# Two-layer hybrid decoder step: norms and combinations tile by tile, ten gather buffers, tokens in five transfers, zeros written later

## The reference

```python
def rms_norm(x, g):
    y = xf * lax.rsqrt(jnp.mean(xf * xf, axis=-1, keepdims=True) + RMS_EPS)
    return (y * g).astype(x.dtype)

# layer 0: h += even_mixer(rms_norm(h, norm_mix_even));  h += hier_moe(rms_norm(h, norm_ffn[0]))
# layer 1: h += odd_mixer(rms_norm(h, norm_mix_odd));    h += hier_moe(rms_norm(h, norm_ffn[1]))
# y = rms_norm(h, norm_final)

def even_mixer(h, ...):      # conv and forgetting attention
    proj = jnp.einsum('ntd,de->nte', h, w_in)      # 1024 -> 2568 columns
    ...                                            # GLU, depthwise conv of width 31, attention
    return jnp.einsum('nte,ed->ntd', mixed, w_out), ...

def hier_moe(h, ...):        # top-1 group of 4, top-2 of its 4 experts, 16 experts in all
    g_logits = x2 @ w_group + b_group              # 4 columns
    e_logits = x2 @ w_router + b_router            # 16 columns
    ...
    for e in range(N_EXPERTS):
        hid = silu(x2 @ w_gate[e]) * (x2 @ w_up[e])
        y = y + combine[:, e:e + 1] * (hid @ w_down[e])
    return y
```

## Time and profile before

| | |
|---|---|
| median of 3 runs | 1676.36 us |
| the profiled execution, and its span | 1680.96 us, 1679.2 us |
| busy: PE, DVE, ACT, POOL | 1415.1, 641.4, 299.0, 144.2 us |
| chain that ended last: PE, DVE, DMA | 55%, 20%, 12% |
| mean granted clock of TensorE | 0.901 |
| transfers | 341.60 MB, 203 GB/s mean |

### The profile page before, as it was taken

One profiled execution on the slowest core, in us unless ns is written; L12 is line 12 of the kernel. 1 busy time (PEld: TensorE's weight loads), 2 busy tenths in 40 slices (PEclk: granted clock), 3 DMA queues, 4 the chain that ended last, 5 costly groups with the idle time before them and its releaser, 6 DMA issues.

```text
span 1679.2 us, 28659 instructions
## 1 busy us (share of the span) xinstructions
PE 1415.1 (84%) x11123; PEld 808.3 (48%) x11124; DVE 641.4 (38%) x1502; ACT 299.0 (18%) x749; POOL 144.2 (9%) x370
## 2 busy tenths in 40 slices
PE   4999957889977999989569987888998699998990
PEld 2444633545464555555254443445645555555550
DVE  2029954322135221111155899567402433111114
ACT  2111023322010000000111211445602000000001
POOL 0039400000000000000110000000000000000002
PEclk9999776989967899999879999799998589999995
DMA  9231107678154699999710022133342277999955
GB/s 347 77 117 51 57 25 227 209 228 311 42 194 156 253 361 391 398 396 410 306 51 29 22 98 77 56 102 101 113 189 105 76 297 269 400 383 394 401 234 183
DMA packets 86587, 341.60 MB, mean 203 GB/s; under 512 B 24743, under 2 KB 32007, under 8 KB 72486
## 3 DMA queue, kind: packets, MB, share of 16 engines
q1 hardware_dynamic: 66254, 289.80, 46.9%
q0 software_dynamic: 10656, 37.56, 6.6%
q10 hardware_dynamic: 9536, 12.33, 2.2%
HBM read 309.53 MB, written 30.47 MB: 202 GB/s over the span
## 4 chain that ended last, share of the span: by engine, by line
PE 55%; DVE 20%; DMA 12%; SPq 4%; issue 4%; ACT 3%; POOL 1%; ACTq 0%; POOLq 0%; DVEq 0%
PE banks L1087 17%; DMA arena<-in_wstream 8%; PE banks L1115 8%; PE banks L1025 7%; DVE arena L2103 6%; PE banks L794 5%; DVE arena L1650 4%; PE banks L825 3%; SPq L440 2%; PE banks L768 2%; DVE arena L1782 2%; DMA arena<-hn_scratch,arena 2%; PE banks L944 1%; DMA arena<-expert_rows,arena 1%; PE banks L753 1%
## 5 line engine op out<-in xcount | busy, mean ns | idle before, releaser
L1087 PE MATMUL banks<-arena 128*32 128x128 f32 (+1 forms) x4736 | 362.4, 338 | 24.2 <-issue 11.7
L1087 PEld LDWEIGHTS banks<-arena 128*32 128x32 f32 (+1 forms) x4736 | 241.6, 127 | 143.8 <-issue 52.6
L1115 PE MATMUL banks<-arena 128*64 128x512 f32 (+1 forms) x1184 | 180.3, 510 | 1.1 <-ACT arena L1529 1.1
L1650 DVE TENSOR_TENSOR arena<-arena,banks 128x256 f32<-128x256 f32 (+5 forms) x84 | 38.9, 464 | 306.9 <-PE banks L1087 175.4
L794 PE MATMUL banks<-arena 128*128 128x512 f32 x320 | 139.3, 595 | 0.0
L2022 DVE COPY arena<-banks 128x256 f32<-128x256 f32 (+1 forms) x56 | 21.4, 381 | 285.1 <-PE banks L1100 278.8
L1650 DVE TENSOR_TENSOR arena<-arena 128x256 f32<-128x256 f32 (+17 forms) x248 | 98.8, 432 | 77.9 <-ACT arena L1394 56.4
L1650 DVE TENSOR_TENSOR arena<-banks,arena 128x512 f32<-128x512 f32 (+5 forms) x159 | 70.4, 473 | 143.5 <-ACT arena L1453 81.5
L825 PE MATMUL banks<-arena 128*128 128x512 f32 x256 | 117.6, 605 | 0.0
L1025 PE MATMUL banks<-arena 128*128 128x512 f32 x256 | 112.5, 601 | 1.4 <-issue 0.8
L2103 DVE SCALAR_TENSOR_TENSOR arena<-arena 128x512 f32<-128x512 f32 x120 | 105.2, 937 | 1.1
(11 more groups left out here) (274 smaller groups left out, 1513.3 us busy)
## 6 DMA issues: line engine op xcount, KB each, us to landing
arena<-in_wstream SPq DMA_DIRECT2D x109, 2048.0 KB, 13.9
arena<-in_fox_kt SPq DMA_DIRECT2D x64, 256.0 KB, 3.0
arena<-in_fox_v SPq DMA_DIRECT2D x64, 256.0 KB, 3.0
arena<-in_dsa_page SPq DMA_DIRECT2D x64, 256.0 KB, 2.9
expert_rows<-arena ACTq DMA_DIRECT2D x76, 128.0 KB, 9.0
expert_rows<-arena POOLq DMA_DIRECT2D x1, 6656.0 KB, 33.2
hn_scratch<-arena POOLq DMA_DIRECT2D x8, 512.0 KB, 3.0
expert_rows<-arena ACTq DMA_DIRECT2D x72, 32.0 KB, 7.1
```

The source lines that it names most:

```text
L1087: last = mm(bank(b, 0, 4 * n, n * j, n * j + n), x[:, c, :], w[:, c, 4 * n * j:4 * n * j + 4 * n], start=(c == 0), stop=(c == DC - 1))
L1115: last = mm(bank(3, 0, 8 * n, n * q, n * q + n), ht2[g % 2][:, 128 * i + n * j:128 * i + n * j + n], w[:, c, 8 * n * q:8 * n * q + 8 * n], ...
L1650: return v.tensor_tensor(out, x, y, op)
```

## The change

- A norm's mean, root and reciprocal are made for each tile apart. ACT loads the table for roots by a root of one unused value ahead of the squares.
- Norms 1 and 3 move into `out_project(l)`: during its second block (b == 1) DVE makes `hn` and `xt` of earlier tiles between the sums, PE turns them between the jobs and does the router's products for them.
- Norm 0 on PE moves into `project_even`: the transposes of tile t+1 stand ahead of the job of tile t in block 0.
- `combine(l)` gathers into ten buffers (in regions CR and X) without waiting for a sum; both rows of a tile are waited for together. DVE's sums, norm 2 and norm 4 are interleaved: tile t is summed, then t-1's mean made, t-2's `hn` (or final product) and t-3's `xt`. PE still turns all five tiles of norm 2 before the first tail product.
- The final product has five buffers instead of two, so it waits for no transfer out.
- The tokens come in five transfers, with the constants and the first ring block among them. The write of zeros goes to after the first gated tile (`u_ready` 1).

```diff
-        def norm(n):
-            for t, c0, c1 in TILES:
-                pe.wait_ge(S(f"hn{n}"), upto(f"hn{n}", t + 1))
...
+        def turn_h(n, t):
+            pe.wait_ge(S(f"hn{n}"), upto(f"hn{n}", t + 1))
+            if t - 1 > 0:
+                pe.wait_ge(S(f"xt{n}"), upto(f"xt{n}", t - 1))
+            for c in range(DC):
...
+            last.then_inc(S(f"hn_t{n}"), 1)
 # project_even
+            pe.wait_ge(S("c_ident"), 16)
+            turn_h(0, 0)
             for b in range(NBLK[0]):
-                pe.wait_ge(S(f"ring{k % RING}"), ring_loads(k))
                 for t, c0, c1 in TILES:
                     if b == 0:
+                        if t < NT - 1:
+                            turn_h(0, t + 1)
                         pe.wait_ge(S("xt0"), t + 1)
+                    if t == 0:
+                        pe.wait_ge(S(f"ring{k % RING}"), ring_loads(k))
 # out_project(l) on PE
                     last.then_inc(S(f"out_mm{l}"), 1)
+                    if b == 1 and t >= 2:
+                        turn_h(2 * l + 1, t - 2)
+                    if b == 1 and t >= 3:
+                        route_tile(l, t - 3)
+            turn_h(2 * l + 1, 3)
+            route_tile(l, 2)
+            turn_h(2 * l + 1, 4)
+            route_tile(l, 3)
+            route_tile(l, 4)
 # norm(n) on ACT
+            af(tick[0], tick[0], ACT.Sqrt)
+            for t in range(NT):
+                square(t)
+                if n in (2, 4):
+                    if t:
+                        root(t - 1)
+                else:
+                    root(t)
 # DVE: out_project(l), then combine(l)
                 last.then_inc(S(f"out_add{l}"), 1)
+                if b == 1 and t >= 1:
+                    mean_square(2 * l + 1, t - 1)
+                    normed(2 * l + 1, t - 1)
+                if b == 1 and t >= 2:
+                    to_xt(2 * l + 1, t - 2)
+            mean_square(2 * l + 1, NT - 1)
+            to_xt(2 * l + 1, NT - 2)
+            normed(2 * l + 1, NT - 1)
+            to_xt(2 * l + 1, NT - 1)
...
+            for t in range(NT + 3):
+                if t < NT:
+                    combine_tile(l, t)
+                if 1 <= t <= NT:
+                    mean_square(n, t - 1)
+                if 2 <= t <= NT + 1 and l == 0:
+                    normed(n, t - 2)
+                if t >= 3 and l == 0:
+                    to_xt(n, t - 3)
+                if 2 <= t <= NT + 1 and l == 1:
+                    final(t - 2)
 # POOL
-                if t - 1 > 0:
-                    pool.wait_ge(S(f"combined{l}"), upto(f"combined{l}", t - 1))
                 for k in range(2):
-                    i = (2 * t + k) % 4
+                    i = 2 * t + k
...
+        pool.wait_ge(S("u_ready"), 1)
         pool.dma_start(y_d[NROWS:, :].rearrange("(s p) d -> p s d", p=128),
                        bc_mid(zeros, SPILLS))\
             .then_inc(S("zeros_out"), 16)
 # SP
+        tokens(0)
         sp.dma_start(ident, a["ident"]).then_inc(S("c_ident"), 16)
         sp.dma_start(at("SMALL", 0, 168), a["small"]).then_inc(S("c_small"), 16)
+        tokens(1)
         stream(0)
+        for t in range(2, NT):
+            tokens(t)
```

More of the change, by code:

```diff
@@ L1627, in _ @@
         spilled(1)
[L1629 to L1636 removed]
+        norm(4)
     @block.vector
@@ L1686, in attend, with to_xt @@
+        def to_xt(n, t):
+            dve.wait_ge(S(f"hn_t{n}"), upto(f"hn_t{n}", t + 1))
+            for k in range(2):
+                src = g3(bank(4 + 2 * (t % 2) + k), 4)[:, :, 0:rows(t)]
+                last = tt(xt[:, 4 * k:4 * k + 4, 128 * t:128 * t + rows(t)], src,
+                          bc_last(gain[n][:, 4 * k:4 * k + 4], rows(t)), ALU.mult)
+            last.then_inc(S(f"xt{n}"), 1)
         def attend(l, chunk0, bias, beside=None):
@@ L2088, in _, with combine_tile @@
-        v.memset(ssq, 1.0).then_inc(S("init"), 1)
-        norm(0)
+        def combine_tile(l, t):
+            hv = h[0:rows(t), t, :]
+            dve.wait_ge(S(f"yb{l}_{t}"), upto(f"yb{l}_{t}", 32))
+            for k in range(2):
+                i = 2 * t + k
+                ins = v.scalar_tensor_tensor(out=hv, in0=ybuf[i][0:rows(t), :],
+                                             scalar=wts[0:rows(t), NT * k + t:NT * k + t + 1], in1=hv,
+                                             op0=ALU.mult, op1=ALU.add)
+                if k == 0:
+                    step(ins)
+            ins.then_inc(S(f"combined{l}"), 1)
@@ L2090, in _ @@
+        dve.wait_ge(S("c_small"), 16)
+        for t in range(NT):
+            mean_square(0, t)
+            normed(0, t)
+            if t:
+                to_xt(0, t - 1)
+        to_xt(0, NT - 1)
         for t in range(NT):
@@ L2340, in _ @@
         combine(1)
-        norm(4)
-        dve.wait_ge(S("c_fin"), 16)
-        for t in range(NT):
-            if t >= 2:
-                dve.wait_ge(S(f"y_out{t % 2}"), 16 * (t // 2))
-            v.scalar_tensor_tensor(out=yfin[t % 2][0:rows(t), :], in0=h[0:rows(t), t, :],
-                                   scalar=rstd[0:rows(t), t:t + 1], in1=fin_g[0:rows(t), :], op0=ALU.mult,
-                                   op1=ALU.mult).then_inc(S("y_ready"), 1)
     ctx.close()
```

150 lines of the change are left out of this document (58 added, 92 removed).

## The result

The changed kernel takes 1636.2 us (median of 4 runs, 1630.0 to 1639.7) against 1676.2 for the kernel before on the same chip: ratio 0.9757 (0.9720 to 0.9793), 40.0 us less, where 36.1 were forecast. In a second comparison, on another chip, the medians were 1644.2 (six runs, 1629.0 to 1646.9) and 1683.9, ratio 0.9728, 39.6 less. (A ratio here is not quite the quotient of the two medians, which is 0.9761 for the first pair.) The profiled execution of the changed kernel is its fastest run, 1629.98 us (span 1628.2); that of before, at 1680.96, lies above all of its timed runs (1674.9 to 1677.8). So these two traces differ by 51.0 us, and 11 of them are no gain of the change.

A forecast was written before the change was run, and what follows sets the result against it. TensorE, busy 1415.1 of 1679.2 us, bounds the kernel, so waits and slow-clock stretches count. Terms -14.3 - 12.5 + 4.4 + 4.8 - 12.5 - 6.0 = -36.1 take 1676.36 to 1640 us, range 1625 to 1658.

The forecast's parts named there:

- Start: Program start: job 0 at 11.9 us, block 1 at 47.9 instead of 62.16, 14.3 us saved.
- The rival with the late block: Start: first weight block still lands near 21.8 us, queued behind tokens; only 4.4 saved there, 1650 in all; chance 0.10.
- Norm 1 and 3 with the router: Output projection to router end, each layer: idle wait gone, some tiles turned and routed before the last job; 12.5 us saved.
- Rival 2: Output projection: first routed tile already lowers the clock, 3.3 us saved a layer instead of 12.5; 1654, chance 0.20.
- the rival that ends slower: Block 0 and output projections: inserted transposes bring the clock down until the projection ends; 1697 us, chance 0.03.
- First gather of layer 0: Experts of layer 0: the earlier gather meets weight blocks in flight, 4.4 us lost, bounds 0 and 4.4.
- Combination, norm 2, tail: Layer 0 behind the experts: tiles turned sooner but tail at slow clock; 4.8 us lost, bounds 8.2 lost, 5.1 saved.
- if the tail takes 8.4 us: 72-column tail behind norm 2: sign that the prediction is wrong, as it expected 15.7 us at slow clock.
- the dense job behind it starts slow, 2.2 more: Dense job behind the 72-column tail: starts at the slow clock, costing 2.2 us more.
- Layer 1's gather at nothing: Experts of layer 1: no keys loaded, order and distance of weight blocks and gather stay, so no gain or loss.
- End: Final combination and products: last product at 1669.4 instead of 1675.8; 6.0 us saved, 4.1 with gathers 2.2 apart.
- Rival 1: Routers and tail: clock holds wherever TensorE is busy, routers 3.3 us sooner, tail 8.4 us; 1624, chance 0.15.

The follow-up runs named there:

- e1_again: The changed kernel run once more without any edit, for a second profile: median 1644.2 us, ratio 0.9728 to the kernel before.
- e3: Changed kernel, but TensorE turns and routes all tiles behind the output projection again, DVE's early norm kept: 1646.4 us, ratio 0.9743 to the kernel before.
- e2: Changed kernel, but SP issues two weight blocks of layer 0's first expert earlier, between the key loads: 1630.0 us, ratio 0.9688 to the kernel before.
- e7_zeros_first: Changed kernel with the 6.5 MB of zeros issued at the start again, tokens still in five transfers: 1644.4 us, ratio 0.9756 to the kernel before.
- e10: Kernel of e2 with the final gain loaded earlier and 14 unused dense products ahead of the tail: 1621.3 us, ratio 0.9673 to the kernel before.
- e5: Kernel of e2 with 14 unused dense products ahead of and between norm 2's turned tiles: 1629.8 us, ratio 0.9665 to the kernel before.
- e6: Kernel of e2 with 16 unused dense products in TensorE's idle time behind each router: 1637.2 us, ratio 0.9708 to the kernel before.
- e4: Changed kernel, but DVE makes all ten sums of a layer before the first mean: 1638.9 us, ratio 0.9729 to the kernel before.

## Why the prediction was right, and where it was off

- **Start, -14.3.** Measured -14.1, job 0 at 11.6 to 13.1 (forecast 11.9), block 1 at 47.9. The reason given was half right: "the zeros no longer share the engines" is 3.6 us of it, together with the tokens 7.8, the order the rest. The 2.5 us for the slow clock behind idle time were 3.0 in e1_again (10.1 us for job 0), nothing in the first profile (7.1) and 1.6 on average of nine. The output projection starts at 393.9 on average, 14.0 sooner than before, so the gain arrives whole and the zeros cost nothing where they now stand. The rival with the late block is out. The Trainium skill (DMA: Bandwidth & Descriptors, "Anatomy of one DMA") would have had the block there at 10.4, an estimate by a fit that it gives for transfers issued by GpSimd; this one, issued by SP and sharing its queue with tokens, landed at 11.7 in the first profile, 1.3 us later.
- **Norm 1 and 3 with the router, -12.5 each.** Measured -12.9 and -13.8. The step on which it rested, the clock at 1.00 for some 5 us behind the last dense job and 0.50 then, showed in both layers, with 7 us in the first profile (4 to 7 in all); the router ended 11.6 us after that job, where I wrote 12. e3 measured what I had not separated: insertion 4, early norm 9. Rival 2, the first routed tile brings the clock down, is out (the job behind it took 3.67), and so is the rival that ends slower.
- **First gather of layer 0, +4.4.** The mechanism was right (12.02 us for this gather, 4.38 for that of layer 1) and the size was not: +7.8, beyond my upper bound. The bound came from a gather beside one or two blocks (8.71 us); this one met three blocks of 2 MB issued within 2 us. I had written that they were in flight past 500 and still priced the gather by the milder row. e2 shows that nearly all of it is the collision.
- **Combination, norm 2, tail, +4.8.** Measured -5.5 in the profiled run, and about +2 in six of nine profiles; -0.7 on average. The step "the tail takes 15.7 instead of 8.4" held where the clock was down (15.6 in these six), and failed in the other three, the profiled run among them, so that one of the prediction's own signs of being wrong ("if the tail takes 8.4 us") appeared: I took the router's stretch as the pattern for 72-column products behind transposes of full width. The term "the dense job behind it starts slow, 2.2 more" was too large in every profile: 3.88 to 4.70 us for its 31 records instead of 3.62, so 0.3 to 1.1. Without it, and with the 5.6 to 6.2 us by which the tail begins sooner (3.4 in e1_again; I had 4.7), the slow case costs about 2.
- **Layer 1's gather at nothing**: 15.42 us against 15.63, right.
- **End, -6.0.** Measured -7.0 between the two first profiles, -8.2 on average of the two of before. The late load of the final gain, 1.47 us, I had not seen: a buffer that moves takes its load's condition along.
- **Rival 1, the clock holds wherever TensorE is busy.** Its time, 1624, was below all runs of the changed kernel. Its claim fails in e1_again, 0.50 through 15.6 us of unbroken work. The Trainium skill (TensorE: Matmul & The Clock Gate, "What's actually happening"), read as busy time, does not tell this tail from the one at 1.00; the trace has both, at 4.00 of 4.00 us busy.

The total was nearer than its terms, -36.1 against -40.0, and that is partly luck. The gather cost 3.4 more than forecast and the stretch behind the tail 3.6, for which there was no term; against them the combination with the tail came out 5.5 better, the end 2.2, the experts 1.7 and norm 3 with its router 1.3.

Open: what of the remaining scatter lies in the experts (295.5 to 305.7 us a layer over 24 stages). Four of these stages, layer 1 of e1_again, layer 0 of e3_behind and both of e7_zeros_first, hold one wait of 6.3 to 6.9 us for gathered rows; they took 304.4 to 305.7, the other twenty 299.8 on average, with no such wait above 3.1. What makes that gather late is not shown. Thinning out the key loads themselves was not tried.

## What to carry to other kernels

When a result comes earlier, look at what its consumer's transfer will now meet in the queues: more than half of the 13 us won at the router of layer 0 were lost to three weight blocks that SP issued when its own list allowed, and came back by moving two issues. Thin products did not raise the clock here in 15.6 us, while dense ones put ahead of them did, so look at the work just ahead. Dense products whose results nobody uses paid here where the engine idled anyway (e10, though not measurably in e5), and did not where they outlasted the wait (e6). And read a term in several profiles before giving it a sign: one trace of before and one of after differed by 11 us more than their kernels.

## What the runs showed of the hardware

- The 80 products with 72 columns took 8.2 us or 15.6 us in the same kernel, always fully busy. At 0.50 they never brought the clock up (seven profiles); at 1.00 they kept it in all but one (e4), where it fell about 2 us into them, behind transposes with gaps. With 20 columns, and full-width transposes between them, the clock fell during the work, 4 to 7 us behind the last dense product.
- Sparse full-width transposes (five sets of 8 in 13 to 16 us) brought the clock up in three of nine profiles; with 14 dense products among them it was up in both profiles.
- A gathered row set took 12.02 us instead of 4.29 when three 2 MB loads had been issued in the 9 us ahead of it, and 7.74 when they had been issued 12.6 us ahead.
- Zeros of 6.5 MB in flight delayed a 2 MB load by some 2.7 us (12.2 instead of 9.5, the mean of 8.8 to 10.3) when 1 MB of tokens stood ahead of it, and with 2.3 MB ahead by 6.3 (18.6 against 12.3): the two delays did not simply add.
